# The first expert group's tokens gathered alone, and its products put ahead of the other groups' gathers

## What is computed

```
biased = sigmoid(h @ w_router) + b_router      # best 4 of 8 groups, then the best 6 experts
combine = the 6 gates of each token, scaled to a sum of 2.5
gu = einsum("td,edf->tef", h, w_expert_gu)      # (384, 64, 512)
act = silu(gu[..., :256]) * gu[..., 256:] * combine
routed = einsum("tef,efd->td", act, w_expert_down)
gs = h @ w_shared_gu
shared = (silu(gs[..., :256]) * gs[..., 256:]) @ w_shared_down
```

## Time and profile before

| | |
|---|---|
| median of 3 runs | 731.2 us (730.85 to 732.66) |
| profiled execution | 730.38 us, of it span 728.4 us |
| TensorE busy | 683.9 us, 94% |
| VectorE, ScalarE, GpSimd busy | 53%, 27%, 12% |
| DMA | 259 MB, mean 356 GB/s; 384 to 428 GB/s in each slice from 273 to 710 us |
| mean granted TensorE clock | 0.989 |

### The profile page before, as it was taken

One profiled execution on the slowest core, in us unless ns is written; L12 is line 12 of the kernel. 1 busy time (PEld: TensorE's weight loads), 2 busy tenths in 40 slices (PEclk: granted clock), 3 DMA queues, 4 the chain that ended last, 5 costly groups with the idle time before them and its releaser, 6 DMA issues.

```text
span 728.4 us, 11392 instructions
## 1 busy us (share of the span) xinstructions
PE 683.9 (94%) x4209; PEld 399.2 (55%) x4209; DVE 388.8 (53%) x1000; ACT 193.3 (27%) x327; POOL 85.3 (12%) x52
## 2 busy tenths in 40 slices
PE   1799999989999999999999999999999999998993
PEld 1689888768856645544444544454445445444431
DVE  3388999695295544454444434454445436442114
ACT  3244334473373311211111111111111121130113
POOL 2445553513201000000000000000000000000000
PEclk9899999999999999999999999999999999999997
DMA  9999866815489469999999999999999999999994
GB/s 323 373 348 331 263 232 232 287 61 173 146 327 422 204 238 420 423 426 422 404 384 425 425 422 424 422 425 424 425 425 425 428 421 427 422 426 423 420 408 176
DMA packets 51012, 259.14 MB, mean 356 GB/s; under 512 B 6704, under 2 KB 9312, under 8 KB 32904
## 3 DMA queue, kind: packets, MB, share of 16 engines
q1 hardware_dynamic: 46816, 252.50, 86.1%
q0 software_dynamic: 1584, 4.90, 2.0%
q10 hardware_dynamic: 2552, 0.98, 0.5%
HBM read 254.64 MB, written 3.71 MB: 355 GB/s over the span
## 4 chain that ended last, share of the span: by engine, by line
PE 71%; DMA 12%; DVE 9%; SPq 4%; issue 2%; ACT 1%; POOL 0%; DVEq 0%; ACTq 0%
PE psum L2365 22%; PE psum L2373 10%; PE psum L2258 9%; PE psum L2337 8%; DMA w_gu<-in_w_expert_gu 7%; PE psum L598 4%; DVE psum L1303 4%; PE psum L600 4%; PE psum L599 4%; PE psum L2239 3%; DMA w_gu<-in_w_ada 3%; DMA w_dn<-in_w_expert_down 2%; SPq L794 1%; PE psum L1980 1%; PE psum L2324 1%
## 5 line engine op out<-in xcount | busy, mean ns | idle before, releaser
L2365 PE MATMUL psum<-w_gu,hgT 128*32 128x512 f32 (+1 forms) x1280 | 191.4, 594 | 2.6 <-DMA w_gu<-in_w_expert_gu 2.6
L2365 PEld LDWEIGHTS psum<-w_gu,hgT 128*32 128x32 f32 (+1 forms) x1280 | 57.7, 119 | 128.0 <-issue 127.9
L1770 DVE TENSOR_TENSOR f_acc<-f_acc,psum 128x512 f32<-128x512 f32 x132 | 86.6, 684 | 43.4 <-PE psum L2337 43.4
L2373 PE MATMUL psum<-w_dn,actT 128*32 128x512 f32 (+1 forms) x640 | 98.7, 596 | 1.4 <-DMA w_dn<-in_w_expert_down 0.9
L1748 DVE SCALAR_TENSOR_TENSOR act<-sil,wsl,psum 128x256 f32<-128x256 f32 x27 | 18.4, 681 | 127.9 <-ACT sil L1104 118.7
L583 POOL TENSOR_TENSOR w_lo<-w_gu,w_hi 128x2048 fp32r<-128x2048 f32 x13 | 59.8, 4600 | 73.8 <-ACT w_hi L874 73.8
L2258 PE MATMUL psum<-onehot,h_lo 128*128 128x512 f32 (+1 forms) x168 | 66.6, 396 | 0.0
L2258 PE MATMUL psum<-onehot,h_hi 128*128 128x512 f32 (+1 forms) x168 | 65.0, 387 | 0.6 <-DVE onehot L1606 0.6
L1754 DVE TENSOR_TENSOR y_lo<-psum,y_hi 128x1024 fp32r<-128x1024 f32 x26 | 31.8, 1223 | 51.2 <-ACT y_hi L1108 51.2
L2373 PEld LDWEIGHTS psum<-w_dn,actT 128*32 128x32 f32 (+1 forms) x640 | 27.0, 119 | 58.5 <-issue 57.7
L1104 ACT ACTIVATE sil<-psum 128x256 f32<-128x256 f32 x27 | 10.4, 384 | 173.8 <-PE psum L2365 173.8
(11 more groups left out here) (317 smaller groups left out, 859.5 us busy)
## 6 DMA issues: line engine op xcount, KB each, us to landing
w_gu<-in_w_expert_gu SPq DMA_DIRECT2D x49, 2048.0 KB, 17.7
w_dn<-in_w_expert_down SPq DMA_DIRECT2D x61, 1024.0 KB, 15.5
w_gu<-in_w_expert_gu SPq DMA_DIRECT2D x27, 1024.0 KB, 15.4
w_gu<-in_w_ada SPq DMA_DIRECT2D x12, 2048.0 KB, 13.5
w_gu<-in_w_in SPq DMA_DIRECT2D x4, 2048.0 KB, 12.8
w_gu<-in_w_out SPq DMA_DIRECT2D x2, 2048.0 KB, 10.1
bc<-mod_rows POOLq DMA_DIRECT2D x6, 512.0 KB, 7.5
w_gu<-in_w_expert_gu SPq DMA_DIRECT2D x6, 512.0 KB, 20.4
```

The source lines that it names most:

```text
L1770: v.tensor_tensor(dst, dst, bank(5 + n), ALU.add).then_inc(f_added, 1)
L2365: ins = t.matmul(bank(target)[rows, :], column(c)[:, rows], w_gu[s][:, c, :], start=(c == 0), stop=(c == NC - 1), tile_position=(0, rows.s ...
L2373: ins = t.matmul(bank(target + n)[rows, :], actT[:, j, rows], w_dn[s][:, j, 512 * n:512 * (n + 1)], start=(j == 0), stop=(j == 1), tile_po ...
```

## The change

The gather of the first batch is split. `first_gather` gathers group 0 alone (128 columns) and waits for a new signal, `first_ready`, which VectorE gives after the one-hots of experts 0 and 1; the same signal, at 2, stands for the gates that `tw_ready` stood for. Group 0's gate and up products wait only for its own eight copies (`g0_ready`). Behind them on TensorE come: the nine slot products, the second shared down product, a wait for VectorE's reading of the slots, the third shared transposes, two chunks of `next_gather` (groups 1 and 2, 256 columns), the third shared down product, group 0's transposes and down products, and then the other six chunks. ScalarE follows that order; the copy of the second shared product (`f_first(1)`) moves behind group 0's silu. On VectorE `make_onehot(1, 0)` moves ahead of the three `tokens_of`.

```diff
--- before.py
+++ after.py
@@ -464,7 +464,8 @@
         f_done, f_added = sem("f_done"), sem("f_added")
-        tw_ready, fhi_ready, flo_ready = sem("tw_ready"), sem("fhi_ready"), sem("flo_ready")
+        g0_done, g0_ready = sem("g0_done"), sem("g0_ready")
+        first_ready, fhi_ready, flo_ready = sem("first_ready"), sem("fhi_ready"), sem("flo_ready")
         oh_ready, slots_done, wsl_ready = sem("oh_ready"), sem("slots_done"), sem("wsl_ready")
@@ -1083,7 +1084,6 @@
             sh_silu(2)
-            f_first(1)
 
@@ -1114,17 +1114,28 @@
 
-            for c in range(2):
-                hgT_evac(0, c)
-            actT_evac(3, actT_s)
-            for c in range(2, NC):
-                hgT_evac(0, c)
+            def first_evac(c):
+                a.wait_ge(g0_done, c + 1)
+                a.activation(hgT[:, c, :], bank(c % 2, 0, P), ACT.Copy).then_inc(g0_ready, 1)
+
+            def next_evac(c):
+                a.wait_ge(hgT_done, c + 1)
+                a.activation(hgT[:, :, :].rearrange("p (g c) q -> p c g q", c=NC)[:, c, 1:3, :],
+                             bank(c % 2, 0, 2 * P).rearrange("p (g q) -> p g q", q=P), ACT.Copy).then_inc(hgT_ready, 1)
+
+            for c in range(NC):
+                first_evac(c)
             a.wait_ge(gate_out, 32)
...
                 gate(k, s_last, loads)
+                if k == 0:
+                    f_first(1)
+                    actT_evac(3, actT_s)
+                    for c in range(2):
+                        next_evac(c)
                 actT_evac(k + (NT + 1), actT)
@@ -1132,6 +1143,9 @@
                     y_high_halves(s_last, loads)
+                if k == 0:
+                    for c in range(2, NC):
+                        next_evac(c)
 
@@ -1617,15 +1631,15 @@
 
-            def first_onehot(j, columns, last=False):
+            def first_onehot(j, columns, last=None):
 
...
                     ins = rows_of(e, onehot[0][:, :, P * j:P * j + P], BLOCK * first, BLOCK * n)
-                    if last and column == columns[-1]:
-                        ins.then_inc(oh_ready, 1)
+                    if last is not None and column == columns[-1]:
+                        ins.then_inc(last, 1)
                     else:
@@ -1634,7 +1648,7 @@
                     if (j, column) == (2, 2):
-                        ins.then_inc(tw_ready, 1)
+                        ins.then_inc(first_ready, 1)
                     else:
@@ -1687,7 +1701,7 @@
             v.wait_ge(x_saved, 16)
-            first_onehot(0, (0, 1))
+            first_onehot(0, (0, 1), last=first_ready)
             v.wait_ge(rank_done, 1)
@@ -1700,7 +1714,7 @@
             first_onehot(1, (1, 2))
-            first_onehot(2, (1, 2), last=True)
+            first_onehot(2, (1, 2), last=oh_ready)
             sh_a(2)
@@ -1714,9 +1728,9 @@
             own.link(v.tensor_tensor(part[:, :], counts, alloc[:, :], ALU.subtract))
+            make_onehot(1, 0)
             for g in range(3):
                 tokens_of(3, g, g, parts_of(g))
-            make_onehot(1, 0)
             v.wait_ge(gate_out, 32)
@@ -2306,16 +2320,31 @@
             transposes(2, act_s)
-            sh_down(1)
+
+            def first_gather(c):
+
+                if c >= 2:
+                    t.wait_ge(g0_ready, c - 1)
+                for n, (i, part) in enumerate(EVERY):
+                    ins = t.matmul(bank(c % 2, 0, P), part[:, i, c, :], onehot[0][:, i, 0:P],
+                                   start=(n == 0), stop=(n == 2 * NT - 1))
+                ins.then_inc(g0_done, 1)
+
+            def next_gather(c):
+
+                if c >= 2:
+                    t.wait_ge(hgT_ready, c - 1)
+                for n, (i, part) in enumerate(EVERY):
+                    ins = t.matmul(bank(c % 2, 0, 2 * P), part[:, i, c, :], onehot[0][:, i, P:3 * P],
+                                   start=(n == 0), stop=(n == 2 * NT - 1))
+                ins.then_inc(hgT_done, 1)
+
             t.wait_ge(hi_ready, NT)
             t.wait_ge(lo_ready, NT)
-            t.wait_ge(oh_ready, 1)
+            t.wait_ge(first_ready, 1)
             t.wait_ge(a_ready, 2)
-            gather(0, 0)
-            gather(0, 1)
-            transposes(3, act_s)
-            for c in range(2, NC):
-                gather(0, c)
+            for c in range(NC):
+                first_gather(c)
 
@@ -2397,10 +2426,6 @@
 
-            t.wait_ge(tw_ready, 1)
-            t.wait_ge(ident_ready, NT)
-            batch_slots(0)
-
             def combines(k):
@@ -2420,7 +2445,9 @@
                 uses, tiles = weights_of(k)
-                if 0 in cs:
+                if k == 0:
+                    t.wait_ge(g0_ready, NC)
+                elif 0 in cs:
                     t.wait_ge(hgT_ready, NC * (b + 1))
@@ -2450,10 +2477,20 @@
 
+                if k == 0:
+                    t.wait_ge(oh_ready, 1)
+                    t.wait_ge(first_ready, 2)
+                    t.wait_ge(ident_ready, NT)
+                    t.wait_ge(actT_ready, 2)
+                    batch_slots(0)
+                    sh_down(1)
+                    t.wait_ge(wsl_ready, 3)
+                    transposes(3, act_s)
+                    for c in range(2):
+                        next_gather(c)
+                    sh_down(2)
                 some_outputs(2)
                 piece(0)
-                if k == 0:
-                    sh_down(2)
                 transposes(k + (NT + 1), act)
```

## The result

The changed kernel takes 732.88 us (median of 16 runs, 731.64 to 736.61) beside 731.37 for the kernel before (16 runs, 729.32 to 732.66). The ratio is 1.0034, 95% interval 1.0022 to 1.0045: 2.5 us slower, between 1.6 and 3.3. The ratio is taken from all runs; the two medians alone lie 1.5 us apart, since the runs of the changed kernel scatter upward. The profiled execution has a span of 730.7 us, 2.3 more than before.

A forecast was written before the change was run, and what follows sets the result against it. The transfer stream sets the end, but TensorE's slot releases set when its last uninterrupted part begins. Path +2.7 and balance +3.1 gave +2.8 us, on 731.2 making 734.0; range 731.2 to 739.5.

The forecast's parts named there:

- rival 1: Split gather: 128-column products go as slowly as plain f32, 0.22 us each; delay 7.9, time 739.1; chance 0.25.
- rival 2: Split gather: narrow products go by columns, 0.058 us at 128, or loads overlap better; delay about 1.0, time 732.2; chance 0.14.
- late down block: Weight refill that waits for the last shared down product; issue forecast at 265.8 us.
- head start: First group's products and first refill come 8.5 us earlier; forecast to be gone by the second refill, the stream 0.5 late.
- Covers: Evacuations with no work beside them: about 0.65 us ahead of the first group, 0.7 ahead of the second.
- the queue's sum: Transfers from 254.4 us stand idle 3.3, 1.8 and 4.0 us; second refill flows from 280.8 instead of 280.3.
- its rival: Head start lives if the queue holds bytes at each refill issue; 722.7 to 729 us, middle 726; chance 0.11.
- The balance: To the second group: gathers +2.7, removed waits -1.1, new waits +1.5, together +3.1 us.
- the path: TensorE's steps summed from the first group's products at 248.8 to the second group at 275.0, 2.7 us later.
- the thin places: Near 355 and 370 us transfers wait for TensorE, losing 1.0 and 1.2 us; there the stream takes the whole delay.

The follow-up runs named there:

- run with the high part only: Changed kernel with the low part of the tokens left out of the gather for the second and third group; 1.0006, +0.4 us against the kernel before.
- padding at the first group: Kernel before with 16 more 384-column products on TensorE between the first group's down products and the second group; 1.0041, +3.0 us.
- runs with the exchanged plan: Fifth group three experts, tenth two: on the kernel before 0.9992 and 0.9996; on the changed kernel 1.0001 and 0.9995; all against the kernel before.
- new order without the split: Kernel before with the change's order behind the first group's products, but all three groups gathered at once; 1.0119, +8.7 us against the kernel before.

## Why the prediction was right, point by point

| step | predicted | profile after |
|---|---|---|
| first gather begins | 242.7 | 243.09 (0.44 of it from before the change) |
| a product of 128 columns | 0.113 (0.22 in rival 1, 0.058 in rival 2) | 0.112 |
| a product of 256 columns | 0.116 | 0.118 |
| first group's products | 248.8 | 249.01 (0.2 early by the common event) |
| first refill issued | 252.6 | 252.85 |
| late down block, two down blocks | 265.8, 270.1 | 265.82, 270.30 |
| second group | 275.0, delay 2.7 | 275.17, delay 2.4 without what lies before the change |
| second refill issued | 279.0 | 278.99 |
| last down weights | some 3 us later | 688.76, 2.3 later (0.44 of it from before the change) |
| time | +2.8, to 734.0 | +2.5 (1.6 to 3.3), median 732.88 |

The change is slower because the split gather puts more work on TensorE ahead of the second group than the removed waits give back; the head start doesn't make up for it, since the next refills find slots that aren't free yet. That was the prediction's mechanism. That the size came out within 0.3 us is partly luck: the measurement itself is known to 0.8, and two small errors, given below, stand in the sum.

*Where the gather's price lay.* The row that decided was the nine slot products of the earlier trace rows: full stationary block, six moving columns, 0.11 us. The narrow products cost nearly that (0.112 at 128 columns, 0.118 at 256), so up to 256 columns the width hardly counts. That it is the load of the block which sets this pace is my reading of these rows; no run changes the block alone. The split therefore costs TensorE 5.4 + 5.6 us where one gather took 8.3. Rivals 1 and 2 fell with this one number. The figure of the Trainium skill for a sustained pair at 128 columns (page "TensorE: Matmul & The Clock Gate", section "Back-to-back issue gap") is 81 ns; for this type the trace has 112, and the prediction was right to leave it out of the sum.

*Covers.* The last evacuation, bare in the change, cost a wait of 0.37 us ahead of the first group and 0.47 ahead of the second (the brackets in the timeline); with drain and first load, counted from where the next product would have begun at the gather's pace, it is 0.53 and 0.63 where I had 0.65 and 0.7. The wait for VectorE's reading of the slots cost nothing, as forecast.

*The head start.* It went as the queue's sum had it: holes where the slots weren't free. The run with the high part only puts a head start of 9 us at no more than 1.2 us; I had given its rival a chance of 0.11.

*The balance.* Beside the path, which gave a delay of 2.7, stood a balance of +3.1, and I took 2.8 between them. The balance counted the removed waits by their brackets (1.1 us) and the new ones with drain and first load. From start to start the two removed ones are 0.7 and 0.8 in the earlier trace rows, and then it gives the path's 2.7. The measured 2.4 is below both: 0.2 at the first group and 0.1 at the last shared down product (3.43 us, not 3.54).

*The term that was a little off.* I passed the whole delay on to the end. In the profile the issues are 2.9 us late at 373.55 and 2.3 at the last down weights (0.44 of each from before the change); TensorE's wait for expert weights fell from 2.6 to 1.9 us. The padding at the first group shows the same (2.6 to 1.9). From the common event to the end the profiles are 1.9 us longer for the change, 2.4 for the padding and 0.4 for the run with the high part only, where the second group is 2.4, 3.0 and 0.95 late: each time 0.5 to 0.6 less than the delay. One sentence was too strong: that the stream is already 2.4 us late by 305 and only the remainder is added near 355. It's late there, but the runs with the exchanged plan show that this lateness costs little, 0.3 us in the mean of two pairs that are each known to about 1.2, as long as the queue doesn't run empty again. The sum was right in its result because at the thin places nearly the whole delay counts, which it said too.

*What stays open.* Full flow in 340 to 380 us should have brought the kernel before 2.2 us; it brought 0.3 to 0.6, and TensorE's waits for transfers fell by 1.1 (3.5 to 2.4). In its profile the transfers issued at 642.0 land 24.0 us later (median), those of the kernel before, issued at 641.8, after 24.7, so what TensorE waits for comes half a microsecond earlier, although the bytes moved are over 2 us ahead. Whether a few of the 16 engines were never idle in the thin places and set each landing, I couldn't see in a view that has only their mean; it isn't shown.

## What to carry to other kernels

When transfers may only be issued as the computing engine frees their buffers, look for the places where the queue runs empty, and price a reordering by how late it makes the issues there; a head start ends at the first release that it can't bring forward. A batched product that is split for latency pays for each stationary block again, and here a narrow product cost as much as one of 256 columns: take its price from the narrowest product in the trace and not by columns. The same lateness is free where the transfers' queue stays full and the computing engine waits for transfers later on, up to the length of those waits: place added work there.

## What the runs showed of the hardware that I had not expected

- After 4.8 us without a product TensorE's next products of 384 columns took 0.33 us instead of 0.17 for over 4 us (granted clock 0.74 in 248 to 256 us of the new order without the split). The change's first gather fills that hole. The Trainium skill, page "TensorE: Matmul & The Clock Gate", section "What's actually happening", has the lower level at 1.2 GHz, half of the upper, and the steps of 0.32 and 0.17 agree with that.
- Rounded (fp32r) products with a full stationary block take 0.112 us at 128 moving columns, 0.118 at 256, 0.174 at 384 and 0.23 at 512 (the last from the gathers of the later batches, 283.22 to 283.45 in the profile after).
- The second shared transposes began between 241.91 and 244.76 us in the profiles of these kernels, whose TensorE program up to there is the same. Single spans differ by that much before the change even begins; a stretch has to be measured from a common event.
